# A mixture-of-experts encoder layer: quarter tiles with signals of their own, and five small stores moved

## The reference, cut to what matters

```python
def step(y, xs):
    toks, ws, e = xs
    xb = h2[toks]
    hb = jax.nn.silu(xb @ w_gate[e]) * (xb @ w_up[e])
    return y.at[toks].add((hb @ w_down[e]) * ws[:, None]), None
```

## Time and profile before

| | us |
|---|---|
| median of three runs | 2656.3 |
| lowest and highest | 2650.55, 2661.9 |
| the profiled execution's own time | 2651.97 |
| its span | 2650.3 |

### The profile page before, as it was taken

How to read it: one execution, slowest core, us unless ns; L and a number is a source line. 1 busy time by engine, 2 the same in 40 slices (tenths; PEclk the granted TensorE clock), 3 DMA queues, 4 the chain that set the end, 5 groups by cost and what they waited for, 6 DMA issues and landing times. The chain is left out here.

```text
span 2650.3 us, 40161 instructions
## 1 busy us (share of the span) xinstructions
PE 2431.2 (92%) x14824; PEld 2183.7 (82%) x14824; DVE 1923.1 (73%) x3073; ACT 1373.6 (52%) x2032; POOL 1339.5 (51%) x1317
## 2 busy tenths in 40 slices
PE   4999999999999999999986999699999999999990
PEld 4889898898998989989875775499989898888980
DVE  7475765757758567575676687578888888888875
ACT  3443625426245263452633332267777777777772
POOL 6354664646546556455564265334555455554320
PEclk9999999999999999999987999799999999999995
DMA  5201111111110111101113323489999999999994
GB/s 183 61 26 33 54 34 45 34 40 46 42 45 28 39 45 39 57 25 41 45 73 115 102 75 134 119 261 285 311 305 310 302 303 311 307 313 313 352 333 162
DMA packets 207582, 380.77 MB, mean 144 GB/s; under 512 B 22694, under 2 KB 129546, under 8 KB 206874
## 3 DMA queue, kind: packets, MB, share of 16 engines
q1 hardware_dynamic: 180330, 302.31, 33.0%
q0 software_dynamic: 25824, 71.42, 11.8%
q10 hardware_dynamic: 1232, 4.46, 0.4%
HBM read 314.84 MB, written 72.97 MB: 146 GB/s over the span
## 5 line engine op out<-in xcount | busy, mean ns | idle before, releaser
L122 PE MATMUL ps<-xTh,w_mix_low 128*128 128x368 f32 (+1 forms) x1728 | 595.8, 345 | 10.2 <-POOL w_mix_low L116 8.8
L123 PE MATMUL ps<-xTl,w_mix_high 128*128 128x368 f32 (+1 forms) x1728 | 569.6, 330 | 0.0
L124 PE MATMUL ps<-xTh,w_mix_high 128*128 128x368 f32 (+1 forms) x1728 | 567.5, 328 | 0.0
L2087 POOL DMA_INDIRECT ys_d<-yo,tab_early x114 | 214.2, 1879 | 426.9 <-DVE yo L2259 263.9
L122 PEld LDWEIGHTS ps<-xTh,w_mix_low 128*128 128x128 f32 x1728 | 326.0, 189 | 21.9 <-issue 18.6
L123 PEld LDWEIGHTS ps<-xTl,w_mix_high 128*128 128x128 f32 x1728 | 326.2, 189 | 9.1 <-issue 6.2
L124 PEld LDWEIGHTS ps<-xTh,w_mix_high 128*128 128x128 f32 x1728 | 325.6, 188 | 0.0
L2129 PE MATMUL ps<-xghl,wgh 128*128 128x320 f32 (+5 forms) x1024 | 271.4, 347 | 13.5 <-DVE xghl L116 6.9
L2129 PE MATMUL ps<-xghl,wuh 128*128 128x320 f32 (+5 forms) x1024 | 263.4, 344 | 0.0
L2131 PE MATMUL ps<-xghl,wgl 128*128 128x160 f32 (+5 forms) x1024 | 240.0, 234 | 0.0
L2131 PE MATMUL ps<-xghl,wul 128*128 128x160 f32 (+5 forms) x1024 | 238.6, 233 | 0.0
(11 more groups left out here) (378 smaller groups left out, 5968.8 us busy)
## 6 DMA issues: line engine op xcount, KB each, us to landing
wd_early<-in_w_exp_down SPq DMA_DIRECT2D x64, 1024.0 KB, 9.2
wg_early<-in_w_exp_gate SPq DMA_DIRECT2D x124, 512.0 KB, 7.5
wu_early<-in_w_exp_up SPq DMA_DIRECT2D x124, 512.0 KB, 5.8
w_mix_raw<-in_w_in SPq DMA_DIRECT2D x72, 512.0 KB, 3.9
mT_d<-gs_m SPq DMA_DIRECT2D x8, 544.0 KB, 2.7
xr_m<-in_x_prompt SPq DMA_DIRECT2D x8, 512.0 KB, 3.7
xn_d<-xr_m SPq DMA_DIRECT2D x8, 512.0 KB, 2.8
out<-vrow_m SPq DMA_DIRECT2D x8, 512.0 KB, 4.8
```

The lines of the kernel that those rows point to most:

```text
L122: pe.matmul(out, ll, rh, start=start, stop=False)
L123: pe.matmul(out, lh, rl, start=False, stop=False)
L124: return pe.matmul(out, lh, rh, start=False, stop=stop)
L2087: pool.indirect_dma_start(out=ys_d[:, :], out_offset=rows_of(e, j, m), in_=yo[:m, b, j, :], in_offset=None, compute_op=ALU.add, bounds_che ...
```

## The change

- Quartered second tiles raise a semaphore pair of their own, `xq_in`; `x_in` counts first tiles and whole second tiles only (`whole_of`). `turn` waits for `x_in` alone, `quarters_turned` for `xq_in`.
- `gather(e)` waits for the quarters of the expert two before, and for their turn, only ahead of its own quarter transfer.
- `quarters_turned(e + 1)` moves on VectorE from ahead of the gate copy of e to behind `hT` of e, directly ahead of `x_low_part(e + 1)`. ScalarE's order is as it was.
- The five stores leave the end of the joint stage, with their wait for `planned`. SyncE issues them in the experts' program, at e = 3, behind the loads of gate and up weights and ahead of that of the down weights, with a wait for `tab_s` instead. `step` and `limit` are stored as one row and spread over the partitions when `overflow` reads them.

```diff
         picks_d = dram("picks_d", [P, NT, TOPK], U32)
         pairs_d = dram("pairs_d", [P, NT * TOPK * 2], U32)
-        step_d, limit_d = dram("step_d", [P, NE]), dram("limit_d", [P, NE])
+        step_d, limit_d = dram("step_d", [1, NE]), dram("limit_d", [1, NE])
 
         def first_experts(stack, suffix):
...
             sp.dma_start(tb[:, :, :].rearrange("e s o -> e (s o)"), tok_d[0:NE * CAP, :].rearrange("(e s) o -> e (s o)", e=NE)) \
                 .then_inc(tb_in, 16)
-            sp.wait_ge(planned, 1)
-            sp.dma_start(plan_d[0:OVB, :], plan[0:OVB, 0:1]).then_inc(kept, 16)
-            sp.dma_start(plan_d[OVB:OVB + 1, :], plan[0:1, 1:2]).then_inc(kept, 16)
-            sp.dma_start(only_d[:, :], only[0:OVB, :]).then_inc(kept, 16)
-            sp.dma_start(step_d[:, :], STEP).then_inc(kept, 16)
-            sp.dma_start(limit_d[:, :], limit[:, :]).then_inc(kept, 16)
             sp.wait_ge(early_in, 16 * 3 * STATIC)
             sp.wait_ge(stored[0], 16 * 5)
...
                                         bounds_check=last_token, oob_is_err=False).then_inc(xi0, 16)
+        return (plan_d[0:OVB, :], plan[0:OVB, 0:1]), (plan_d[OVB:OVB + 1, :], plan[0:1, 1:2]), (only_d[:, :], only[0:OVB, :]), \
+            (step_d[:, :], num[0:1, 2, :]), (limit_d[:, :], limit[0:1, :])
...
     quartered = [0 < n <= QUAD for n in second]
     quarters = [sum(quartered[:e]) for e in range(NE + 1)]
+    quarters_of = [[sum(quartered[r] for r in range(b, e, 2)) for e in range(NE + 1)] for b in range(2)]
+    whole_of = [[of_buffer[b][e] - quarters_of[b][e] for e in range(NE + 1)] for b in range(2)]
 
     GB, UB, TB, DB = 0, 2, 5, (4, 1, 2, 3)
...
         (gu_part, gu_sum, gi0, gi1, ui0, ui1, di0, di1, t_done, x_high, x_low, gh, gl, uh, ul, dh, dl,
                 g_done, u_done, s_done, h_s, h_high, h_done, d_done, y_ready, w_ready, st0, st1, h2_clear,
-                u_part, y_merged, ahead_in, q_done) = sems
+                u_part, y_merged, ahead_in, q_done, xq0, xq1) = sems
         kept, yo0, yo1, xi0, xi1, h2_stored0, h2_stored1, y_left, y_right, x_clear, tab_s = both
-        y_out, x_in = (yo0, yo1), (xi0, xi1)
+        y_out, x_in, xq_in = (yo0, yo1), (xi0, xi1), (xq0, xq1)
         g_in, u_in, d_in, stored = (gi0, gi1), (ui0, ui1), (di0, di1), (st0, st1)
         high, low = (gh, uh, dh), (gl, ul, dl)
...
                         sp.wait_ge(low[which], e + 1)
                         load(which, e + 2)
+                if e == 3:
+                    sp.wait_ge(tab_s, 4)
+                    for dst, src in late_stores:
+                        sp.dma_start(dst, src).then_inc(kept, 16)
                 if 1 <= e < NE - 1:
                     sp.wait_ge(low[DOWN], e)
...
                 b = e % 2
                 if e >= 2:
-                    pool.wait_ge(x_in[b], 16 * of_buffer[b][e])
+                    pool.wait_ge(x_in[b], 16 * whole_of[b][e])
                     pool.wait_ge(t_done, e - 1)
-                    if quartered[e - 2]:
-                        pool.wait_ge(q_done, quarters[e - 1])
                 if quartered[e] and not quarters[e]:
                     pool.wait_ge(tab_s, 5)
                 for j, m in row_tiles(e):
                     if j and quartered[e]:
+                        if quartered[e - 2]:
+                            pool.wait_ge(xq_in[b], 16 * quarters_of[b][e])
+                            pool.wait_ge(q_done, quarters[e - 1])
                         pool.indirect_dma_start(out=xg[:, b, 1, 0:D // 4], out_offset=None,
                                                 in_=h2_d[:, :].rearrange("t (q n) -> (t q) n", q=4),
                                                 in_offset=bass.IndirectOffsetOnAxis(ap=tabq[:, e:e + 1], axis=0),
-                                                bounds_check=last_quarter, oob_is_err=False).then_inc(x_in[b], 16)
+                                                bounds_check=last_quarter, oob_is_err=False).then_inc(xq_in[b], 16)
                         continue
                     pool.indirect_dma_start(out=xg[:m, b, j, :], out_offset=None, in_=h2_d[:, :],
...
             def turn(e):
                 b, c2 = e % 2, second[e]
-                pe.wait_ge(x_in[b], 16 * of_buffer[b][e + 1])
+                pe.wait_ge(x_in[b], 16 * whole_of[b][e + 1])
                 if e:
                     pe.wait_ge(x_low, upto[e])
...
                     return
                 b = e % 2
-                dve.wait_ge(x_in[b], 16 * of_buffer[b][e + 1])
+                dve.wait_ge(xq_in[b], 16 * quarters_of[b][e + 1])
                 dve.wait_ge(x_high, upto[e])
                 dve.wait_ge(x_low, upto[e])
...
                 if e:
                     low_part(dve, DOWN, e - 1)
-                if e + 1 < NE:
-                    quarters_turned(e + 1)
 
                 dve.wait_ge(g_done, e + 1)
...
                 dve.tensor_tensor(hT[:, 0:2 * cap], sl[:, 0:2 * cap], up[:, 0:2 * cap], ALU.mult).then_inc(h_s, 1)
                 if e + 1 < NE:
+                    quarters_turned(e + 1)
                     x_low_part(e + 1)
                 dve.wait_ge(h_high, upto[e + 1])
...
             @block.sync
             def _(sp):
-                for dst, src in ((dest[:, :, :], dest_d[:, :, :]), (picks[:, :, :], picks_d[:, :, :]), (step[:, :], step_d[:, :]),
-                                 (limit[:, :], limit_d[:, :]),
+                for dst, src in ((dest[:, :, :], dest_d[:, :, :]), (picks[:, :, :], picks_d[:, :, :]), (step[:, :], step_d[0].partition_broadcast(P)),
+                                 (limit[:, :], limit_d[0].partition_broadcast(P)),
                                  (pairs[:, :, :, :].rearrange("p t k o -> p (t k o)"), pairs_d[:, :])):
                     sp.dma_start(dst, src).then_inc(lin, 16)
```

More of the change, by code:

```diff
@@ L195, in build @@
             ns, nb = len(SHARED_SEMAPHORES.split()), len(BRIDGE_SEMAPHORES.split())
-            bridge(nc, block, sems[:ns], sems[ns:ns + nb], a, ps, ident, ones, before, st, woh, wol, mT_d, xn_d, h2_d, ys_d, tok_d, plan_d,
+            late_stores = bridge(nc, block, sems[:ns], sems[ns:ns + nb], a, ps, ident, ones, before, st, woh, wol, mT_d, xn_d, h2_d, ys_d, tok_d, plan_d,
                    gates_d, only_d, dest_d, picks_d, pairs_d, step_d, limit_d, place, order, early)
@@ L203, in build @@
                 ("sl", [P, 2 * CAP]), ("yo", [P, 2, 2, D]))]
-            ahead = experts(nc, block, sems[:ns], sems[ns + nb:], a, ps, ident, h2_d, ys_d, order, tab, tabw, tabq, bufs)
+            ahead = experts(nc, block, sems[:ns], sems[ns + nb:], a, ps, ident, h2_d, ys_d, order, tab, tabw, tabq, bufs, late_stores)
         overflow(nc, a, ps, ident, h2_d, ys_d, tok_d, plan_d, gates_d, only_d, dest_d, picks_d, pairs_d, step_d, limit_d, bufs)
@@ L1353 @@
 EXPERT_SEMAPHORES = ("x_gu_part x_gu_sum x_g_in0 x_g_in1 x_u_in0 x_u_in1 x_d_in0 x_d_in1 x_t_done x_x_high x_x_low x_gh x_gl x_uh x_ul x_dh x_dl "
-                     "x_g_done x_u_done x_s_done x_h_s x_h_high x_h_done x_d_done x_y_ready x_w_ready x_st0 x_st1 x_h2_clear x_u_part x_y_merged x_ahead_in x_q_done")
+                     "x_g_done x_u_done x_s_done x_h_s x_h_high x_h_done x_d_done x_y_ready x_w_ready x_st0 x_st1 x_h2_clear x_u_part x_y_merged x_ahead_in x_q_done x_xq0 x_xq1")
 def bridge(nc, block, both, sems, a, ps, ident, ones, before, st, woh, wol, mT_d, xn_d, h2_d, ys_d, tok_d, plan_d, gates_d, only_d, dest_d,
@@ L1942, in _, with experts @@
                                         bounds_check=last_token, oob_is_err=False).then_inc(xi0, 16)
-def experts(nc, block, both, sems, a, ps, ident, h2_d, ys_d, order, tab, tabw, tabq, bufs):
+        return (plan_d[0:OVB, :], plan[0:OVB, 0:1]), (plan_d[OVB:OVB + 1, :], plan[0:1, 1:2]), (only_d[:, :], only[0:OVB, :]), \
+            (step_d[:, :], num[0:1, 2, :]), (limit_d[:, :], limit[0:1, :])
+def experts(nc, block, both, sems, a, ps, ident, h2_d, ys_d, order, tab, tabw, tabq, bufs, late_stores):
     wg, wu, wd, xg, sl, yo = bufs
```

## The result

The changed kernel took 2659.2 us (median of 20 runs, 2656.3 to 2666.8), the kernel before, run beside it, 2654.0 us (20 runs): a ratio of 1.0022, with a 95% interval of 1.0015 to 1.0028. It is 5.2 us slower. The profiled execution took 2659.2 us, with a span of 2657.5.

A forecast was written before the change was run, and what follows sets the result against it. It took a closed VectorE-ScalarE loop of 13.94 us per quartered expert, without TensorE, as the bound. Loop growth +10.3 and stalls -5.5 gave +4.8 us on the 2656.3 median: 2661 us, range 2646 to 2675.

The forecast's parts named there:

- the loop's growth: VectorE-ScalarE loop: each 32-row quarter tile adds 0.31 us to the expert's period, +10.3 us over all such tiles.
- the stalls' gain: Waits for two late quarter tiles, 3.4 us the longest, vanish from the loop: -5.5 us.
- the stores' gain: Five stores moved off SyncE ahead of the first gather: counted at nothing, with a gain only as bound.
- The bound: Quartered experts: 6.94 us of VectorE, then 7.00 us of ScalarE, make the whole 13.94 us period; TensorE follows.
- TensorE sets the pace: Rival: TensorE bounds the experts, so the extra 0.31 us hides and only the stall goes: 2651 us, chance 0.15.
- Steps 1 to 3: Moved turn: VectorE gains 0.60 us, ScalarE's high part of hT comes 0.91 later; over 39 tiles +10.3 us.
- the slower rival: Gate copy on VectorE can't start earlier, so the 0.60 us is not regained: 2684.5 us, chance 0.12.
- Step 5: Own quarter signals, and VectorE asking for the quarter 4.0 us later, remove stalls of late quarter tiles: -5.5 us.
- Step 6: GpSimd: the turn ends about 2010.15, before the quarter's gather could be issued at 2010.46, so no cost.
- Step 7: Five stores moved from behind planned to expert 3 on SyncE: no cost and no gain counted.
- a sign that I am wrong: TensorE's wait ahead of the first transposes falling well below 11.3 us would show the prediction wrong.

The follow-up runs named there:

- the second: The changed kernel measured once more as a control, with nothing altered, beside the kernel before: 2657.8 us, ratio 1.0009 (0.9996 to 1.0022).

## Why the prediction was right, and where it was not

The forecast was 2661 us, 4.8 above the kernel before; measured were 2659.2 and 5.2 above by the medians of the first measurement, and 4.5 by those of the second (by the ratios 5.8 and 2.4). Sign and size hold, and the term that decides the sign, the loop's growth, was right in mechanism and nearly in size. That the sum fits to 1 us is luck: the stalls' gain was put too large and the stores' gain at nothing, and these two errors offset each other.

1. The bound, a loop of VectorE and ScalarE without TensorE: right. The turn put back, the doubled high part and ScalarE's order each moved the period by what the loop says, while TensorE's work stayed the same, 13.72 us where it ran without a gap. The rival "TensorE sets the pace" is out.
2. Steps 1 to 3, +10.3 us: predicted 0.31, 0.25 and 0.20 us per expert, measured 0.32, 0.28 and 0.24, and 0.37 in the period that I counted at nothing, where the first quarter tile is turned: 11.5 us in the profiles. The 0.60 us came back at the gate copy (2.81 to 2.21 us) and 0.56 of it at `hT`, so the slower rival had no ground. I had said that the gate's products would be there in time.
3. Step 5, -5.5 us: the stalls did vanish, in all nine profiles with the turn behind `hT`. The cause is the later turn, as step 5 had it beside the signals; signals of their own do nothing by themselves, and where they are missing the late quarter holds TensorE by up to 1.4 us and no period grows. The size was taken from one profile. The four profiles with the turn in its old place have 5.7, 1.2, 1.6 and 3.5 us of stalls, 3.0 on average.
4. Step 6: no cost, as found, but my reason was mistaken. The turn that GpSimd waits for lies a whole period back, not just ahead of the gather; its margin is an expert, not 0.3 us.
5. Step 7, nothing: this failed. The moved stores take 3 to 5 us off the time ahead of the first transposes (7.7 to 9.8 us against 4.8 to 5.0) by the profiles; the stores alone gave 4.5 us. The wait ahead of the first transposes fell from 11.3 to 6.3 us, which I had named as a sign that I am wrong, and on this step I was: the idle microsecond before the gather was no ground for counting nothing.

With the measured terms the sum is 11.5 - 3.0 - 4.5 = +4.0 us, against 5.2 and 4.5 in the two measurements. The forecast's own sum had a loop term that was too small by 1.2 and a stall term that was too large by 2.5, and it lacked a store term of 4.5.

## What to carry to other kernels

Where two engines hand work to each other once per round, add up the loop before moving an instruction: the step that runs in the idle stretch of one of them is free only as long as its input is early, and moving its producer behind the hand-over puts it, and the wait for it, in the loop. If the producer must move, change the order on the consumer too; here that one edit took 17 us off the changed kernel by the periods and 19 by the medians. A stall seen in one profile is a sample, so its size belongs in the range and not in the sum at full weight.

## What the runs showed of the hardware that I had not expected

Some small stores, through by the profile some 1 to 4 us before a first indirect gather was issued, went with a gather that came into use 2.6 to 5.0 us later (7.7 to 9.8 us after its issue against 4.8 to 5.0), in five profiles against eight. In the kernel before its packets were slow, 1.67 us against 0.50, while the DMA engines moved nothing else. Idle DMA engines ahead of a transfer are no proof that what came before has no part in its time.
